# Layer norms before tensor-multiplied units: low parts of input tiles 6 and 7 moved from VectorE to GpSimd

## The chip, the core and the metric

One NeuronCore of a Trainium2 chip runs the whole program. The metric is the device time in microseconds from the first to the last instruction of one execution, with what lies around it; less is better. The kernel before takes 1235.99 us, the median of three runs (1234.67 to 1236.5).

## What is computed

Three transformer layers on a sequence of 256 tokens of width 1024, in float32. The first layer uses RMS norms. The other two are "hybrid" layers that use layer norms, and these are what the change touches:

```python
def layer_norm(x, g, b):
    mu = jnp.mean(xf, axis=-1, keepdims=True)
    var = jnp.mean(jnp.square(xf - mu), axis=-1, keepdims=True)
    y = (xf - mu) * lax.rsqrt(var + LN_EPS)
    return (y * g + b)

def hybrid_layer(x, ...):
    proj = x @ w_in                       # 38 column tiles with the branch merges
    ...
    x = layer_norm(ALPHA * x + mix, ln1_g, ln1_b)
    up = causal_dwconv_2(x @ w_up, ffn_conv_w)
    a, b = jnp.split(up, 2, axis=-1)
    ffn = (silu(a) * b) @ w_down
    return layer_norm(ALPHA * x + ffn, ln2_g, ln2_b)
```

With two such layers there are four layer norms: `ln10`, `ln20` (first hybrid layer), `ln11`, `ln21` (second). The output of the first three feeds a matrix product; `ln21` is the program's output.

## The kernel before

**Layout and precision.** Activations are held transposed: eight tiles (t = 0 to 7) of 128 features x 256 tokens. TensorE multiplies in a reduced float32 format, so every operand is split into a high part (the value rounded) and a low part (the rest), and one 128 x 128 weight block times one activation tile is three matmuls: high x high (L1065), high weights x low activations (L1066), low weights x high activations (L1067). A "unit" is one 512 KB weight tile of eight such blocks, so 24 matmuls.

**The weight stream.** For every unit SP issues the DMA into a ring of three raw buffers, ScalarE makes the high part (`hi_part`, L733), VectorE the low part (`lo_part`, L1391), and TensorE waits for `split_lo`. The DMA of unit n waits for the low part of unit n - 3. Each engine runs a program order written out by hand; semaphores link them.

**A layer norm.** VectorE makes deviations, ScalarE squares them, GpSimd adds them up, TensorE sums over features and spreads mean and inverse deviation over the partitions, with some matmuls on a tile of ones (`warm`, L1081) between. GpSimd then adds the mean to tiles 1 to 7 of `dev` (L694), tile by tile. VectorE follows in `layer_norm`: for s = 0 to 9 it scales tile s with gain and inverse deviation (L1457, semaphore `scaled`) and then makes the low part of tile s - 2, that is `dev + b - high` (L1461 and its continuation, semaphore `x_lo`). ScalarE makes the high parts `dev + b` (L767, `x_hi`). After its loop VectorE goes on to the low part of the next weights (the third unit of the stage), which ScalarE has made ready beforehand.

**What follows it on TensorE.** `ramp` takes the first two units of the next stage together, tile by tile: for each tile k it waits for the low part of tile k (`LOW[which, k]`), then issues the six matmuls of both units. From the third unit on it waits for weights alone.

**What follows it on GpSimd.** `keep` makes the biased tiles `x = dev + b` (L700), which the residual of the next half layer needs much later. For `ln10` and `ln11` the stage after is the FFN's up projection. There GpSimd has to multiply gate and value of every pair of units (L634, semaphore `product`), and ScalarE, in program order, makes the high part of that product (L993) before it makes the high part of the weights of the sixth unit. So the first product stands behind `keep` on GpSimd, and the sixth unit's weights stand behind the first product on ScalarE. For `ln20` the next stage is `win21`, where GpSimd's next step is `pool_sums`, after the copy of the eighth unit.

For the RMS norms GpSimd already makes the low parts of tiles 4 and 6 (`POOL_LOW`, `low_parts`, L667).

Of the kernel before, what the change touches and what calls it, by code (L numbers as in the profile page):

```python
# [12 lines left out]
KT = DM // P  # L13
# [181 lines left out]
def build(nc, args, out):  # L195
    f32, r32, i32 = mybir.dt.float32, mybir.dt.float32r, mybir.dt.int32
    ALU, ACT = mybir.AluOpType, mybir.ActivationFunctionType
    ctx = ExitStack()
    with ctx:
        def sb(name, shape, dt=f32, stack=ctx):  # L200
            return stack.enter_context(nc.sbuf_tensor(name, shape, dt))

        def sem(name):
            return ctx.enter_context(nc.semaphore(name))
# [11 lines left out]
        def tiles_of(n, at_line):  # L216

            out = []
            for t in range(n):
                which = 0 if t in at_line else 1  # L220
                out.append((aligned, shifted)[which][:, placed[which], :])
                placed[which] += 1
            return out
# [6 lines left out]
        xhi, xlo = tiles_of(KT, (0,)), tiles_of(KT, (0,))  # L230
        yhi, ylo = tiles_of(16, (2, 8)), tiles_of(16, (2, 8))
        x = sb("x", [P, KT, S])
# [45 lines left out]
        def statistic(c, n=2):  # L278
            return stats[:, c:c + n]


        def col(name, i=0, n=1):
            a = COLS[name] + i
            return vec[:, a:a + n]

        def cst(name, n):
# [27 lines left out]
        normed_dve, normed_act, x_hi, x_lo, x_lo_pool = (sem(n) for n in ("normed_dve", "normed_act", "x_hi", "x_lo", "x_lo_pool"))  # L314
# [3 lines left out]
        dev_summed, mean_ready, mean_spread, mean_copied, var_ready, recentred, recentred_dve, mean_squared, x_kept = (  # L318
            sem(n) for n in ("dev_summed", "mean_ready", "mean_spread", "mean_copied", "var_ready", "recentred", "recentred_dve", "mean_squared",
                             "x_kept"))  # L320
# [151 lines left out]
        XHI = {n: KT * i for i, n in enumerate(NORMS)}  # L472
# [4 lines left out]
        LNI = {"ln10": 0, "ln20": 1, "ln11": 2, "ln21": 3}  # L477
        RES = {"ffn": 0, "final": KT, "ln10": 2 * KT, "ln20": 3 * KT, "ln11": 4 * KT, "ln21": 5 * KT}


        POOL_LOW = (4, 6)
        NORMED, LOW, tally = {}, {}, {}

        def tell(s):
            tally[s.name] = tally.get(s.name, 0) + 1
            return s, tally[s.name]

        def dve_last(t):

            return t % 2 == 1  # L490

        for n in NORMS:
            for t in range(KT):
                if n not in LNI:
                    NORMED[n, t] = tell(normed_dve)
                elif n == NORMS[-1]:
                    NORMED[n, t] = tell(normed_dve if dve_last(t) else normed_act)
                if n != NORMS[-1]:
                    LOW[n, t] = tell(x_lo_pool if n not in LNI and t in POOL_LOW else x_lo)

        def square_place(t, it):

# [47 lines left out]
        def _(pool):  # L550
# [112 lines left out]
            def low_parts(which, src):  # L663
                for t in POOL_LOW:
                    pool.wait_ge(*NORMED[which, t])
                    pool.wait_ge(x_hi, XHI[which] + t + 1)
                    pool.tensor_tensor(xlo[t], src[:, t, :], xhi[t].bitcast(f32), ALU.subtract).then_inc(x_lo_pool, 1)  # L667

            def add_squares(which):

                for t in range(FIRST_SUMMED if which == "mix" else KT - 1):
                    if which == "mix":

                        pool.wait_ge((squared, dve_squared)[t % 2], t // 2 + 1)
                    else:
                        pool.wait_ge(squared, SQ[which] + t + 1)
                    add_tile(t, 0, dev[:, t, :], dev[:, 0, :], added_q, ACCQ[which])
# [17 lines left out]

            def keep(which):

                for t in range(KT):
                    pool.wait_ge(scaled, KT * LNI[which] + t + 1)
                    pool.tensor_scalar(x[:, t, :], dev[:, t, :], col(which[:3] + "_b" + which[3], t), None, ALU.add).then_inc(x_kept, 1)  # L700

            add_squares("mix")
            low_parts("mix", dev)
# [8 lines left out]
            for l in range(LAYERS2):  # L712
                for n in range(START[f"win2{l}"], START[f"wout2{l}"]):
                    steps(n)
                merge(KT * (1 + l), 1)
                layer_norm(f"ln1{l}")
                keep(f"ln1{l}")
                ffn(1 + l, f"up2{l}")
                layer_norm(f"ln2{l}")
                if l < LAYERS2 - 1:  # L720
                    keep(f"ln2{l}")
# [654 lines left out]
        def _(dve):  # L1376
            count = [0]

            def link(ins):

                count[0] += 1
                ins.then_inc(dve_chain, 1)
                dve.wait_ge(dve_chain, count[0])
# [13 lines left out]
            def on_diagonal(i, c, done):  # L1397

                for h in range(2):
                    ins = dve.tensor_scalar(diag[:, i, h * P:(h + 1) * P], ident, statistic(c + h, 1), None, ALU.mult)  # L1400
                ins.then_inc(done, 1)

            def invert(which, after=None):
                dve.wait_ge(rooted, SUM[which])
                link(dve.reciprocal(statistic(INVERSE), statistic(DEVIATION)))
                on_diagonal(1, INVERSE, inverted)
                if after is not None:
                    lo_part(after)
                if which in LNI:
                    dve.wait_ge(mean_copied, LNI[which] + 1)  # L1410
                    dve.tensor_tensor(dev[:, 0, :], dev[:, 0, :], mean_rows, ALU.add).then_inc(recentred_dve, 1)  # L1411

                dve.wait_ge(spread, SUM[which])

            def low_part(which, t, src):
                if t in POOL_LOW:
                    return
                dve.wait_ge(x_hi, XHI[which] + t + 1)
                dve.wait_ge(*NORMED[which, t])
                low(xlo[t], src[:, t, :], xhi[t], x_lo)  # L1420
# [19 lines left out]
            def layer_norm(which, last):  # L1440
                i = LNI[which]
                dve.wait_ge(dev_summed, i + 1)
                link(dve.tensor_scalar(statistic(NMEAN), dev_sums, -1.0 / DM, None, ALU.mult))
                on_diagonal(0, NMEAN, mean_ready)
                dve.tensor_tensor(statistic(MEAN2), statistic(NMEAN), statistic(NMEAN), ALU.mult).then_inc(mean_squared, 1)
                dve.wait_ge(mean_squared, i + 1)
                dve.wait_ge(summed, SUM[which])
                dve.scalar_tensor_tensor(statistic(VAR), square_sums, 1.0 / DM, statistic(MEAN2), ALU.mult, ALU.subtract).then_inc(var_ready, 1)
                invert(which)
                g, b = which[:3] + "_g" + which[3], which[:3] + "_b" + which[3]  # L1450
                for s in range(KT + 2):
                    if s < KT:
                        if s == 0:
                            dve.wait_ge(recentred_dve, i + 1)
                        else:
                            dve.wait_ge(recentred, (KT - 1) * i + s)
                        dve.scalar_tensor_tensor(dev[:, s, :], dev[:, s, :], col(g, s), spread_inverse, ALU.mult, ALU.mult).then_inc(scaled, 1)  # L1457
                    t = s - 2
                    if t >= 0 and not last:
                        dve.wait_ge(x_hi, XHI[which] + t + 1)  # L1460
                        dve.scalar_tensor_tensor(xlo[t], dev[:, t, :], col(b, t), xhi[t].bitcast(f32), ALU.add, ALU.subtract) \  # L1461
                            .then_inc(x_lo, 1)
                    if last and s >= 1 and s <= KT and dve_last(s - 1):
                        dve.wait_ge(scaled, KT * i + s)
                        dve.tensor_scalar(x[:, s - 1, :], dev[:, s - 1, :], col(b, s - 1), None, ALU.add).then_inc(normed_dve, 1)  # L1465
# [298 lines left out]
            for n in range(WIN1):  # L1764
                if 24 <= PLAN1[n] < 32:

                    t = PLAN1[n] - 24
# [14 lines left out]
            for l in range(LAYERS2):  # L1782
                lo_part(START[f"win2{l}"] + 2)
                waiting, base = None, KT * (1 + l)
                for p, (kind, t) in enumerate(PLAN2):
                    n = START[f"win2{l}"] + p
# [128 lines left out]
```

## Time and profile before

| | |
|---|---|
| median of three runs | 1235.99 us |
| the profiled execution | 1236.2 us, of which the span of instructions is 1234.4 us |
| TensorE matmul busy | 1208.5 us (98%) |
| TensorE weight load busy | 1183.6 us (96%) |
| VectorE busy | 844.7 us (68%) |
| ScalarE busy | 705.9 us (57%) |
| GpSimd busy | 399.6 us (32%) |
| granted TensorE clock, mean | 0.992 |

A timeline row gives the start in us from the span's start, the duration, engine, line, operation, output and inputs, the count of merged instructions, and in brackets the idle time of the engine ahead of it and what released it. Merged rows (x2 and more) span from the first start to the last end. Starts overlap the end of the instruction before on the same engine a little, since engines are pipelined.

### The profile page before, as it was taken

Reading aid. Unit: us, or ns where it says so; the run is one execution under the profiler, and the core shown is the slowest. Engines: PE = TensorE matmul, PEld = TensorE weight load, DVE = VectorE, ACT = ScalarE, POOL = GpSimd, SP = SyncE. Lnnn points to the kernel's source line nnn. Section 1 sums busy time; section 2 is a strip of 40 time slices with the busy share of each in tenths; the row PEclk is TensorE's granted clock in tenths of the full one; section 3 lists DMA queues with packets and bytes.
Section 4 is the critical chain, followed back from the end, with each engine's and each line's share of the span. In section 5 each row is a group of like instructions: output and inputs, shape, how many; then the busy total and the mean of one; then the engine's idle time right before and its main releaser. Section 6 shows DMA issues by size and latency. Waiting matters only on the chain. (4 is left out here: it accounts for less than half of the span.)

```text
span 1234.4 us, 27264 instructions
## 1 busy us (share of the span) xinstructions
PE 1208.5 (98%) x10242; PEld 1183.6 (96%) x10242; DVE 844.7 (68%) x1458; ACT 705.9 (57%) x1228; POOL 399.6 (32%) x376
## 2 busy tenths in 40 slices
PE   8999999999999999999999999999999999999997
PEld 8998989999999999999999999999999999999997
DVE  5867664676777765767677777755766677777655
ACT  4666566545666654466455666644466555666642
POOL 2006214023334402210338434314610339343313
PEclk8999999999999999999999999999999999999999
DMA  6554445665566666454653666565554654566662
GB/s 242 187 166 142 137 133 153 194 191 169 172 188 197 189 192 189 154 158 151 188 174 123 186 187 198 173 205 155 154 171 142 187 180 128 186 190 187 199 190 87
DMA packets 60288, 212.70 MB, mean 172 GB/s; under 512 B 6688, under 2 KB 7968, under 8 KB 60064
## 3 DMA queue, kind: packets, MB, share of 16 engines
q1 hardware_dynamic: 60192, 211.39, 55.8%
q8 instruction: 65, 1.06, 0.4%
q14 instruction: 31, 0.25, 0.1%
HBM read 210.31 MB, written 1.05 MB: 171 GB/s over the span
## 5 line engine op out<-in xcount | busy, mean ns | idle before, releaser
L1391 DVE TENSOR_TENSOR wlo<-raw,whi 128x1024 fp32r<-128x1024 f32 (+1 forms) x400 | 489.5, 1225 | 302.0 <-ACT whi L733 300.0
L1065 PE MATMUL bank<-shifted,whi 128*128 128x256 f32 x2296 | 639.3, 278 | 1.3 <-POOL shifted L667 1.1
L1066 PE MATMUL bank<-shifted,whi 128*128 128x256 f32 x2296 | 636.2, 277 | 0.0
L1067 PE MATMUL bank<-shifted,wlo 128*128 128x256 f32 x2296 | 635.9, 277 | 0.0
L733 ACT ACTIVATE whi<-raw 128x1024 fp32r<-128x1024 f32 (+1 forms) x400 | 415.7, 1040 | 146.7 <-PE bank L1067 134.4
L1065 PEld LDWEIGHTS bank<-shifted,whi 128*128 128x128 f32 x2296 | 431.5, 188 | 3.1 <-POOL shifted L667 1.3
L1067 PEld LDWEIGHTS bank<-shifted,wlo 128*128 128x128 f32 x2296 | 431.7, 188 | 0.0
L1066 PEld LDWEIGHTS bank<-shifted,whi 128*128 128x128 f32 x2296 | 431.1, 188 | 0.0
L634 POOL TENSOR_TENSOR fprod<-ugate,uval 128x256 f32<-128x256 f32 x66 | 99.4, 1506 | 210.1 <-DVE uval L1736 204.5
L1065 PE MATMUL bank<-fhi,whi 128*128 128x256 f32 x528 | 146.1, 277 | 0.0
L1067 PE MATMUL bank<-fhi,wlo 128*128 128x256 f32 x528 | 145.8, 276 | 0.0
L1066 PE MATMUL bank<-flo,whi 128*128 128x256 f32 x528 | 145.8, 276 | 0.0
L648 POOL TENSOR_TENSOR u<-u,tmp 128x256 f32<-128x256 f32 x48 | 53.6, 1118 | 235.8 <-DVE tmp L1691 233.7
L1065 PE MATMUL bank<-aligned,whi 128*128 128x256 f32 x334 | 105.5, 316 | 5.6 <-DVE wlo L1391 3.8
L1065 PEld LDWEIGHTS bank<-fhi,whi 128*128 128x128 f32 x528 | 99.2, 188 | 0.1
L1066 PEld LDWEIGHTS bank<-flo,whi 128*128 128x128 f32 x528 | 99.1, 188 | 0.0
L1067 PEld LDWEIGHTS bank<-fhi,wlo 128*128 128x128 f32 x528 | 99.1, 188 | 0.0
L1067 PE MATMUL bank<-aligned,wlo 128*128 128x256 f32 x334 | 93.3, 279 | 0.0
L1066 PE MATMUL bank<-aligned,whi 128*128 128x256 f32 x334 | 92.5, 277 | 0.0
L993 ACT ACTIVATE fhi<-fprod 128x256 f32 (+1 forms) x66 | 27.6, 418 | 99.8 <-POOL fprod L634 99.8
L1065 PEld LDWEIGHTS bank<-aligned,whi 128*128 128x128 f32 x334 | 62.8, 188 | 16.1 <-issue 8.2
L1066 PEld LDWEIGHTS bank<-aligned,whi 128*128 128x128 f32 x334 | 62.9, 188 | 0.7
(212 smaller groups left out, 1276.4 us busy)
## 6 DMA issues: line engine op xcount, KB each, us to landing
raw<-in_w_win SPq DMA_DIRECT2D x140, 512.0 KB, 3.6
raw<-in_w_up SPq DMA_DIRECT2D x132, 512.0 KB, 3.6
raw<-in_w_down SPq DMA_DIRECT2D x48, 448.0 KB, 3.8
raw<-in_w_merge SPq DMA_DIRECT2D x32, 512.0 KB, 3.9
raw<-in_w_out SPq DMA_DIRECT2D x24, 512.0 KB, 3.6
raw<-in_w_down SPq DMA_DIRECT2D x24, 512.0 KB, 3.6
x<-in_x SPq DMA_DIRECT2D x4, 256.0 KB, 4.6
rgw<-in_rg_w SPq DMA_DIRECT2D x1, 1024.0 KB, 9.8
```

The lines of the kernel that those rows point to most:

```text
L634: pool.tensor_tensor(tile(fprod, t % 3), tile(ugate, t % 3), tile(uval, t % 3), ALU.mult).then_inc(product, 1)
L648: ins = pool.tensor_tensor(m, m, branch_part(base, t, branch), ALU.add)
L733: act.activation(whi[:, n % RING, 0:blocks * P], raw[:, n % RING, 0:blocks * P], ACT.Copy).then_inc(split_hi, 1)
L993: act.activation(tile(fhi, t, it, 3), tile(fprod, t % 3), ACT.Copy).then_inc(f_hi, 1)
L1065: pe.matmul(ps, whi[:, slot, w], hi, start=first, stop=False)
L1066: pe.matmul(ps, whi[:, slot, w], lo, start=False, stop=False)
L1067: return pe.matmul(ps, wlo[:, slot, w], hi, start=False, stop=last)
L1391: dve.tensor_tensor(wlo[:, n % RING, w], raw[:, n % RING, w], whi[:, n % RING, w].bitcast(f32), ALU.subtract) \
```

## The change

A pair of tiles, `KEPT_FIRST = (6, 7)`, gets its low parts on GpSimd in the three layer norms that feed units. `keep` takes tiles 6 and 7 first, then 0 to 5. For 6 and 7 it waits for its own biased tile (`x_kept`) and for ScalarE's high part (`x_hi`), and subtracts. VectorE leaves out its two instructions for these tiles. TensorE's `ramp` waits for `x_lo_pool` instead of `x_lo` at k = 6 and k = 7; the table `LOW` is built to match.

```diff
         POOL_LOW = (4, 6)
+        KEPT_FIRST = (6, 7)
...
-                    LOW[n, t] = tell(x_lo_pool if n not in LNI and t in POOL_LOW else x_lo)
+                    LOW[n, t] = tell(x_lo_pool if t in (KEPT_FIRST if n in LNI else POOL_LOW) else x_lo)
...
             def keep(which):
 
-                for t in range(KT):
+                for t in KEPT_FIRST + tuple(range(KEPT_FIRST[0])):
                     pool.wait_ge(scaled, KT * LNI[which] + t + 1)
                     pool.tensor_scalar(x[:, t, :], dev[:, t, :], col(which[:3] + "_b" + which[3], t), None, ALU.add).then_inc(x_kept, 1)
+                    if t in KEPT_FIRST:
+                        pool.wait_ge(x_kept, KT * LNI[which] + KEPT_FIRST.index(t) + 1)
+                        pool.wait_ge(x_hi, XHI[which] + t + 1)
+                        pool.tensor_tensor(xlo[t], x[:, t, :], xhi[t].bitcast(f32), ALU.subtract).then_inc(x_lo_pool, 1)
...
                     t = s - 2
-                    if t >= 0 and not last:
+                    if t >= 0 and not last and t not in KEPT_FIRST:
                         dve.wait_ge(x_hi, XHI[which] + t + 1)
                         dve.scalar_tensor_tensor(xlo[t], dev[:, t, :], col(b, t), xhi[t].bitcast(f32), ALU.add, ALU.subtract) \
                             .then_inc(x_lo, 1)
```

## Rows read from the trace of the kernel before

**Rows 1.** The page, part 1: busy time of each engine over the span.
```profile
PE 1208.5 (98%) x10242; PEld 1183.6 (96%) x10242; DVE 844.7 (68%) x1458; ACT 705.9 (57%) x1228; POOL 399.6 (32%) x376
```
**Rows 2.** Timelines of PE, and last of PEld, behind ln10, 670 to 684 us.
```profile
672.49 0.28 PE L1065 MATMUL bank<-shifted,whi 128*128 128x256 f32 x1
...
673.20 0.28 PE L1065 MATMUL bank<-shifted,whi 128*128 128x256 f32 x1
...
673.90 0.28 PE L1065 MATMUL bank<-aligned,whi 128*128 128x256 f32 x1
...
683.69 0.19 PEld L1065 LDWEIGHTS bank<-aligned,whi 128*128 128x128 f32 x1 [1.34 <-DVE wlo L1391]
```
**Rows 3.** Timeline of DVE, same stretch: two scalings, low parts, three weight splits.
```profile
669.97 0.47 DVE L1457 SCALAR_TENSOR_TENSOR dev<-dev,vec,bank 128x256 f32<-128x256 f32 x1
...
671.15 1.26 DVE L1461 SCALAR_TENSOR_TENSOR shifted<-dev,vec,shifted 128x256 fp32r<-128x256 f32 x3
672.34 1.21 DVE L1391 TENSOR_TENSOR wlo<-raw,whi 128x1024 fp32r<-128x1024 f32 x1
...
675.21 1.49 DVE L1391 TENSOR_TENSOR wlo<-raw,whi 128x1024 fp32r<-128x1024 f32 x1
...
682.41 1.22 DVE L1391 TENSOR_TENSOR wlo<-raw,whi 128x1024 fp32r<-128x1024 f32 x1 [2.02 <-ACT whi L733]
```
**Rows 4.** Timelines of POOL, same stretch, in windows that single its instructions out.
```profile
664.11 5.66 POOL L694 TENSOR_TENSOR dev<-dev,fprod 128x256 f32<-128x256 f32 x7 [3.13 <-ACT fprod L748]
...
671.73 2.53 POOL L700 TENSOR_SCALAR x<-dev,vec 128x256 f32<-128x256 f32 x1
...
675.15 0.92 POOL L700 TENSOR_SCALAR x<-dev,vec 128x256 f32<-128x256 f32 x1
...
676.05 1.44 POOL L700 TENSOR_SCALAR x<-dev,vec 128x256 f32<-128x256 f32 x1
...
678.38 1.90 POOL L700 TENSOR_SCALAR x<-dev,vec 128x256 f32<-128x256 f32 x1
...
680.24 0.73 POOL L634 TENSOR_TENSOR fprod<-ugate,uval 128x256 f32<-128x256 f32 x1
```
**Rows 5.** Timeline of ACT, same stretch: first product's high part, then sixth unit's weights.
```profile
681.01 0.42 ACT L993 ACTIVATE fhi<-fprod 128x256 fp32r<-128x256 f32 x1 [2.43 <-POOL fprod L634]
681.33 1.04 ACT L733 ACTIVATE whi<-raw 128x1024 fp32r<-128x1024 f32 x1
```
**Rows 6.** Timeline of POOL, 892 to 893 us: two instructions linked by a semaphore.
```profile
892.09 0.80 POOL L581 TENSOR_TENSOR u<-pads 64x256 f32<-64x256 f32 x1
892.97 4.28 POOL L587 TENSOR_TENSOR u<-pads,const 64x256 f32<-64x256 f32 x3
```
**Rows 7.** Timeline ahead of ln10, 657 to 660 us: POOL beside a weight split.
```profile
657.21 0.75 POOL L661 TENSOR_TENSOR acc<-acc,dev 128x256 f32<-128x256 f32 x1
...
657.46 1.57 DVE L1391 TENSOR_TENSOR wlo<-raw,whi 128x1024 fp32r<-128x1024 f32 x1 [0.74 <-ACT whi L733]
...
657.90 1.72 POOL L661 TENSOR_TENSOR acc<-acc,tmp 128x256 f32<-128x256 f32 x1
```
**Rows 8.** Timelines of POOL behind ln20: keep and its next work.
```profile
864.13 11.55 POOL L700 TENSOR_SCALAR x<-dev,vec 128x256 f32<-128x256 f32 x8
...
887.69 4.33 POOL L577 TENSOR_TENSOR pads<-pads 128x542 f32<-128x542 f32 x3 [11.86 <-ACT pads L1040]
```
**Rows 9.** Timelines behind ln11: POOL's keep, and PEld at the sixth unit.
```profile
1038.05 10.59 POOL L700 TENSOR_SCALAR x<-dev,vec 128x256 f32<-128x256 f32 x8
...
1052.06 0.19 PEld L1065 LDWEIGHTS bank<-aligned,whi 128*128 128x128 f32 x1 [1.26 <-DVE wlo L1391]
```
**Rows 10.** Windows: stretch, its length, busy us of PE, PEld, DVE, ACT, POOL, PEclk, DMA.
```profile
662.00:663.00 1.00, 1.00 (x5) 0.91 (x6) 0.35 (x3) 0.15 (x1) 0.00 (x0) 0.50 0.09 33
682.00:684.00 2.00, 0.85 (x7) 0.66 (x7) 1.59 (x2) 2.00 (x5) 0.00 (x0) 1.00 0.28 113
700.00:850.00 150.00, 149.68 (x1302) 149.21 (x1301) 100.48 (x139) 84.18 (x134) 50.82 (x46) 1.00 0.63 190
```

## Prediction

> **What bounds the kernel now.** I read the page's busy times first: TensorE's matmuls are busy for 98% of the span [rows 1], so only what stops TensorE counts. The busy shares by stretch say where it does not stop: between 700 and 850 us it is busy 149.68 of 150 us [rows 10], so nothing there gives a delay back. It stops around the norms. Then I read the timelines of the three places that the change touches (behind ln10 at 665 us, ln20 at 860 us, ln11 at 1034 us), engine by engine. In the ramp, tiles 6 and 7 are not what TensorE waits for: it begins k = 6 at 672.49 us, k = 7 at 673.20 and the third unit at 673.90, 0.70 us apart [rows 2], which is six matmuls back to back. VectorE's last low parts end at 672.41 (1.26 us from 671.15) and the weight split for the third unit at 673.55 [rows 3], 0.35 us before TensorE wants it. The stop that is left comes later: at the sixth unit TensorE is idle for 1.34 us until 683.69, by its weight load [rows 2], because the split at 682.41 waited for ScalarE [rows 3], ScalarE waited 2.43 us for GpSimd's first product [rows 5], and GpSimd had been in `keep` until 680.24 [rows 4]. The same stands behind ln11, with 1.26 us until 1052.06 [rows 9]. So GpSimd is the engine on the path in two of the three places, and it is the one that gets more work.
>
> **What is removed.** Two of VectorE's eight low parts per norm, 0.39 us each by the pitch of the three in 1.26 us [rows 3]: its next split begins at 671.54 instead of 672.34 and ends at 672.75. This moves nothing: TensorE wants it at 673.90 and had it in time already. What the earlier end could release is the DMA of a later unit, whose buffer is filled long before use. Gain: nothing. Were the 0.35 us of slack not there, it would be worth at most 0.8 us for each of three norms.
>
> **What is added to the ramp.** Tiles 6 and 7 now come from GpSimd, in a chain of four instructions. For ln10:
> - GpSimd is free at 669.77 (5.66 us from 664.11 [rows 4]), but has to wait for tile 6 scaled, at 670.44 (669.97 + 0.47 [rows 3]). Start 670.5: 0.7 us idle that `keep` did not have while it began with tile 0.
> - Biased tile 6: 0.92 us, the length of a `keep` instruction that nothing disturbs (675.15 [rows 4]), so until 671.4. ScalarE's high part is made in the meantime.
> - A dependent instruction starts 0.08 us after the end of the one before (892.09 + 0.80 to 892.97 [rows 6]): 671.5.
> - The subtraction takes 0.73 us undisturbed, like the product [rows 4]. But VectorE is then in a low part and starts its weight split right behind it, at 671.54. How GpSimd fares beside it: an addition begun at 657.90, inside a split that ran from 657.46 to 659.03, took 1.72 us and ended 0.59 us behind it [rows 7]; the `keep` instruction of 671.73 took 2.53 us and ended 0.71 behind the split [rows 3, 4]. So it ends about 0.65 us after 672.75: 673.4.
> - Biased tile 7 until 674.3, 0.08 us, subtraction until 675.1. Nothing of VectorE with two inputs in SBUF runs then, since its next split hangs on TensorE's first unit.
> - TensorE starts k = 6 at 673.5 and k = 7 at 675.2 instead of 673.20: **2.0 us late**, in two stops of about 1.0 us.
>
> Bounds: with no disturbance at all the chain ends at 674.0 (670.5 + 2 x (0.92 + 0.08 + 0.73)), 0.9 us late. With another 1.0 us of blocking in the second pair it is 3.0. I take 2.0 since the split's start is fixed by VectorE's own order.
>
> A rule speaks to the one step I am least sure of. Rows 7 show both orders: the addition of 657.21, begun ahead of the split, took its 0.75 us and the split was stretched to 1.57; the one begun inside it waited. The Trainium skill, "SBUF — State Buffer", section "Who interferes with whom", says that a VectorE instruction with two SBUF inputs and a GpSimd one that reads SBUF exclude each other and that the first to start keeps the port pair. By that rule, a subtraction that gets in before 671.54 ends at 672.2 and VectorE waits; the low part that VectorE is in at 671.5 speaks for the other order here. The `keep` of 671.73 started before its split and was held all the same, which fits only if it was already waiting behind low parts.
>
> **ln20.** The same chain; GpSimd starts `keep` at 864.13 there and is busy with it for 11.55 us [rows 8], against 10.5 behind ln10. Nothing behind it depends on `keep`: GpSimd is idle for 11.86 us before its next real work [rows 8], which hides the longer loop; were that cover gone, its 2.4 us would count. TensorE's 2.0 us stay: **+2.0 us**.
>
> **ln10 and ln11, up to the sixth unit.** Here two shifts meet, and the later one counts. TensorE itself comes 2.0 us late, less the stop of 1.3 us that it had: +0.7. Against this stands GpSimd's first product. From the last subtraction (675.1, call it E) come six `keep` instructions at a pitch of 0.90 and then the product. VectorE's fourth unit split follows TensorE's first unit: before, it came 2.0 us behind k = 7 (673.20 to 675.21 [rows 2, 3]), so now at E + 2.1, and the fifth one 3.0 us later, E + 5.1. One begun just ahead of a split passes unharmed and the next waits (675.15 with 0.92 us, then 676.05 with 1.44, beside the split of 675.21 [rows 3, 4]). So: three instructions until E + 2.7, the fourth held until E + 4.1, two more until E + 5.9, the product held by the fifth unit's split until E + 7.15: 682.25. Before, it ended at 680.97 (680.24 + 0.73). That is 1.3 us later, and product, high part, weights' high part, split and TensorE follow each other without a gap [rows 5, 3, 2]. **+1.3 us each**, of which the 0.7 is a part. If the product itself is not held: +0.8. By plain addition (0.7 idle + 2 x 0.08 + 2 x 0.73, with as much holding as before, where three instructions lost 1.6, 0.5 and 1.0 us [rows 4]) it is 2.3, and 2.8 with one hold more.
>
> **Sum.** 2.0 + 1.3 + 1.3 = 4.6 us on the profiled execution's 1236.2, so 1240.8; that execution lies 0.2 above the median of the runs, so **1240.6 us**, +0.37%. Other queues are untouched: no DMA is issued or moved, ScalarE's order is the same. Readers of the biased tiles come a whole stage later.
>
> **Rivals.**
> - **The subtraction slips in before the split** (the point that decides is whether it starts before about 671.5, or GpSimd's four instructions run with no hold). Then the ramp is 0.9 us late; in ln10 and ln11 this is inside the old stop of 1.3, and if the product is also not later than before, they cost 0 to 0.3. Sum 0.9 to 1.5 us: 1237.1 us, not slower by more than 0.2%. For it: 657.21 [rows 7]. Against: 0.7 us of waiting for tile 6 puts the start beside VectorE's back to back work. It would take the good case in all three. Chance 0.13.
> - **GpSimd's loop counts in full.** The product is 2.3 to 2.8 us late, since the holds fall badly, as they did before. Sum 2.0 + 2 x 2.5 = 7.0: 1243.0 us. For it: three holds in 10.5 us before. Chance 0.22.
> - **The clock falls in the ramp's two stops.** In the norm's thin stretch it was at 0.50, 1.2 GHz, in 662 to 663 us [rows 10]. Against: the stop at 682 to 684, with TensorE busy 0.85 of 2 us, left it at 1.00. Were a fall to last 4 us (an estimate, four such stretches), it would lose 2.0 us behind ln20; behind ln10 and ln11 GpSimd's lateness covers much of it. Sum 4.6 + 2.0 + 2 x 0.6 = 7.8: 1243.8 us. Chance 0.09.
> - **VectorE's earlier end is worth something** that these rows don't show and GpSimd is in time: three times 0.3 us saved, 1235.1. Chance 0.03.
>
> **How the numbers follow.** My forecast has 0.53. The measurement can tell 0.2%, about 2.5 us, from no change, so the border is 1238.5. Slower: the forecast, less 0.02 for its low end, and the two dearer rivals, 0.82. Within: 0.13 + 0.02 and what of the last rival stays inside, 0.16. Faster by over 0.2%: 0.02. Range: from 1237.8 (between the first rival and the ramp's lower bound with small product delays) to 1244.2 (beyond both dear rivals' centres).
>
> **What the profile after would show.** Right: in the ramps TensorE idle twice for about 1 us, at k = 6 and k = 7, released by GpSimd's new subtraction; a first subtraction of 1.7 us or more; GpSimd's first product ending about 1.3 us later and the stop at the sixth unit still there, 0.6 longer than the ramp leaves room for. Wrong: no wait of TensorE for GpSimd in the ramp, a first subtraction of 0.73 us, or a stop at the sixth unit as short as before with the product in its old place. If the product moves by 2.5 us, the placing of the holds was wrong; if the granted clock is under 1 behind the ramp, the clock's rival is true.

## The result

| | us |
|---|---|
| before, median of 7 runs | 1235.99 (1234.67 to 1237.78) |
| changed, median of 7 runs | 1239.79 (1238.31 to 1241.30) |
| ratio | 1.0036, 95% interval 1.0026 to 1.0045 |
| span of the profiled executions | 1234.4 and 1236.5 |

The change costs 3.8 us by the medians, 3.2 to 5.6 us by the interval. The forecast was 4.6 us. The first lines of the changed kernel's page hardly show it (they answer to [rows 1]; the last line is from the page's list of costliest groups):

```profile
PE 1207.5 (98%) x10242; PEld 1181.5 (96%) x10242; DVE 843.6 (68%) x1452; ACT 706.5 (57%) x1228; POOL 400.4 (32%) x382
...
L1070 PE MATMUL bank<-shifted,whi 128*128 128x256 f32 x2296 | 639.2, 278 | 6.0 <-POOL shifted L705 4.5
```

Busy times are the same within 2.1 us; what is new is idle time ahead of a matmul, with GpSimd's new line L705 as what ended it.

### The profile page after: what moved, and what is told of

Its sections match the earlier page's. It is cut to its first block and busy times, and to the rows that moved or that the text cites. A ratio compares the mean times of both kernels' runs of the same rounds, so it can differ in the third digit from the quotient of the medians.

```text
span 1236.5 us, 27270 instructions
## 1 busy us (share of the span) xinstructions
PE 1207.5 (98%) x10242; PEld 1181.5 (96%) x10242; DVE 843.6 (68%) x1452; ACT 706.5 (57%) x1228; POOL 400.4 (32%) x382
```

## Where the time went, read in the trace

**How the stretches are compared.** The two spans differ by 2.1 us and not by 3.8, since single executions also differ where the code is the same. The changed one is 2.0 us ahead already at `ln10`'s first sum (658.4 us against 660.4), which lies before all that the change touches; I have not looked for the reason. A further 1.0 us comes from the three thin stretches from a norm's first sum to its first scaling, 4.58, 4.66 and 4.57 us against 5.28, 5.28 and 4.24: where the granted clock stays at 1.00 such a stretch takes 4.2 us, where it falls to 0.50, up to 5.3. So I don't compare absolute times, but times from one fixed point, the start of VectorE's scaling of tile 6 (L1457 before, L1462 after). It is ahead of all that the change touches.

VectorE behind `ln10` in the changed kernel, the answer to [rows 3]:

```profile
667.32 0.47 DVE L1462 SCALAR_TENSOR_TENSOR dev<-dev,vec,bank 128x256 f32<-128x256 f32 x1
...
668.50 0.48 DVE L1466 SCALAR_TENSOR_TENSOR shifted<-dev,vec,shifted 128x256 fp32r<-128x256 f32 x1
668.89 1.22 DVE L1396 TENSOR_TENSOR wlo<-raw,whi 128x1024 fp32r<-128x1024 f32 x1
...
681.05 1.23 DVE L1396 TENSOR_TENSOR wlo<-raw,whi 128x1024 fp32r<-128x1024 f32 x1 [1.12 <-ACT whi L738]
```

Two low parts are gone; the split for the third unit starts 1.57 us behind the scaling of tile 6 instead of 2.37 [rows 3]. GpSimd in the same stretch, the answer to [rows 4]:

```profile
667.89 1.10 POOL L701 TENSOR_SCALAR x<-dev,vec 128x256 f32<-128x256 f32 x1 [0.77 <-DVE dev L1462]
669.07 1.62 POOL L705 TENSOR_TENSOR shifted<-x,shifted 128x256 fp32r<-128x256 f32 x1
670.68 0.92 POOL L701 TENSOR_SCALAR x<-dev,vec 128x256 f32<-128x256 f32 x1
671.68 0.72 POOL L705 TENSOR_TENSOR shifted<-x,shifted 128x256 fp32r<-128x256 f32 x1
672.38 6.02 POOL L701 TENSOR_SCALAR x<-dev,vec 128x256 f32<-128x256 f32 x6
678.37 1.25 POOL L635 TENSOR_TENSOR fprod<-ugate,uval 128x256 f32<-128x256 f32 x1
```

The reader sees the whole chain of the forecast: 0.77 us idle for tile 6, the biased tile, 0.08 us, a subtraction of 1.62 us that ends 0.58 us behind the split (669.07 + 1.62 against 668.89 + 1.22), then a pair that nothing disturbs, its subtraction in 0.72 us. The first biased tile takes 1.10 us and not the 0.92 of the forecast; this costs nothing, since the subtraction is held until the split is over in either case. Six `keep` instructions take 6.02 us, one of them held, and the product 1.25, held by a split. TensorE's weight loads that had to wait, behind `ln10`, `ln20` and `ln11` (answers to [rows 2] and [rows 9]):

```profile
670.75 0.19 PEld L1070 LDWEIGHTS bank<-shifted,whi 128*128 128x128 f32 x1 [0.97 <-POOL shifted L705]
672.46 0.19 PEld L1070 LDWEIGHTS bank<-shifted,whi 128*128 128x128 f32 x1 [0.96 <-POOL shifted L705]
679.08 0.19 PEld L1070 LDWEIGHTS bank<-aligned,whi 128*128 128x128 f32 x1 [0.36 <-DVE wlo L1396]
682.33 0.19 PEld L1070 LDWEIGHTS bank<-aligned,whi 128*128 128x128 f32 x1 [0.43 <-DVE wlo L1396]
...
865.80 0.19 PEld L1070 LDWEIGHTS bank<-shifted,whi 128*128 128x128 f32 x1 [0.96 <-POOL shifted L705]
867.51 0.19 PEld L1070 LDWEIGHTS bank<-shifted,whi 128*128 128x128 f32 x1 [0.94 <-POOL shifted L705]
...
1043.15 0.19 PEld L1070 LDWEIGHTS bank<-shifted,whi 128*128 128x128 f32 x1 [0.95 <-POOL shifted L705]
1044.86 0.19 PEld L1070 LDWEIGHTS bank<-shifted,whi 128*128 128x128 f32 x1 [0.95 <-POOL shifted L705]
1051.47 0.19 PEld L1070 LDWEIGHTS bank<-aligned,whi 128*128 128x128 f32 x1 [0.38 <-DVE wlo L1396]
1054.72 0.19 PEld L1070 LDWEIGHTS bank<-aligned,whi 128*128 128x128 f32 x1 [0.43 <-DVE wlo L1396]
```

Each ramp has two new stops of 0.94 to 0.97 us, at tiles 6 and 7. Behind `ln10` and `ln11` the old stop of 1.34 and 1.26 us at the sixth unit is now 0.43, with 0.36 and 0.38 at the fifth (behind `ln11` the kernel before had 0.32 there already): the stop moved ahead, and the sixth unit's weights came later all the same.

The table gives, for each kernel's profiled execution, the start of a unit's first weight load less the start of the scaling of tile 6, in us (for the changed kernel's sixth unit behind `ln10`: 682.33 - 667.32 = 15.01).

| kernel | ln10: third | ln10: sixth | ln20: third | ln20: fifth | ln11: third | ln11: sixth |
|---|---|---|---|---|---|---|
| before | 3.82 | 13.72 | 3.76 | 10.03 | 3.75 | 13.78 |
| changed | 5.84 | 15.01 | 5.83 | 12.09 | 5.82 | 15.00 |
| ln20_only | 3.77 | 13.77 | 5.84 | 12.20 | 3.82 | 13.71 |
| ups_only | 5.83 | 15.01 | 3.82 | 10.18 | 5.99 | 15.77 |
| order_only | 3.77 | 14.67 | 3.75 | 10.02 | 3.77 | 14.68 |
| no_lows | 3.82 | 12.99 | 3.75 | 10.01 | 3.76 | 12.93 |
| split_waits | 5.51 | 15.65 | 5.50 | 11.85 | 5.51 | 15.66 |
| keep_later | 3.75 | 12.46 | 3.74 | 10.04 | 3.76 | 12.49 |
| change_keep_later | 5.83 | 14.60 | 5.81 | 12.07 | 6.01 | 15.65 |

Changed less before: 1.29 at the sixth unit behind `ln10`, 2.06 at the fifth behind `ln20`, 1.22 at the sixth behind `ln11`, together 4.6 us.

This is not yet the cost up to the next norm. From the scaling of tile 6 to the next norm's first sum the three stages take 186.13, 168.44 and 184.56 us, before 184.84, 165.00 and 183.88: 1.29, 3.44 and 0.68 us longer, together 5.4. So 1.4 us are added behind `ln20` after the fifth unit, about 0.5 each at the fourteenth and the twenty-fifth, and 0.5 us are given back behind `ln11`. The 1.4 us are not in every execution: in `ln20_only`, with the same code in that stage, it takes 167.24 us, 2.2 more than before. What adds them is not settled.

## The experiments

### One norm or two at a time

`ln20_only` and `ups_only` are the changed kernel with the pair of tiles given by norm. `ln20_only` is shown; in `ups_only` the names are `ln10` and `ln11`. The table `LOW` and `keep` ask the same function:

```diff
+        def kept_first(which):
+            return KEPT_FIRST if which in ('ln20',) else ()
...
-                    if t >= 0 and not last and t not in KEPT_FIRST:
+                    if t >= 0 and not last and t not in kept_first(which):
```

> The change in the norm before win21 alone; ln10 and ln11 as before. My theory: GpSimd's chain of four stops TensorE twice in that ramp, about 1.0 us each, and nothing behind it takes this back, so +2.0 us in total and 2.0 us more from the scaling of tile 6 to the third unit's first matmul (3.87 us before). Rival, that a ramp's delay is partly taken back by slack further on in the stage: under 1 us in total. Rival, that only the up projections cost: 0.

Measured: 1237.58 us against 1235.34 for the kernel before on the same chip, ratio 1.0016 (1.0006 to 1.0026), so 2.2 us by the medians. The third unit behind `ln20` is 2.08 us later, the fifth 2.17, and the other norms are as before. Up to the next norm's first sum the stage is 2.2 us longer (167.24 against 165.00 us), so nothing is given back. The rivals of under 1 us and of 0 fall by the trace; by the time alone 0.7 us would still be inside the interval.

> The change in ln10 and ln11 alone. My theory: each costs 1.3 us at the sixth unit, since GpSimd's first product comes that much later and the ramp's 2.0 us fall into the old stop of 1.3; +2.6 us in total; from the scaling of tile 6 to the sixth unit's first weight load 15.0 us where it was 13.7. Rival, that the ramps' delays count in full: 2 x 2.0 = 4.0 us.

Measured: 1236.85 us, ratio 1.0015 (1.0006 to 1.0025), 1.5 us by the medians; the 2.6 us of my theory are inside the interval (0.7 to 3.1). The sixth unit behind `ln10` is at 15.01, as expected, though the third is 2.01 us late: the ramp's delay is swallowed by the old stop, and the product's is what is left. The rival (4.0 us) is outside the interval. Behind `ln11` it is at 15.77, and the reason is the clock. The windows of this kernel behind its two stops there (stretch, length, busy us of PE, PEld, DVE, ACT, POOL, PEclk, DMA share, GB/s):

```profile
1042.00:1043.00 1.00, 0.91 (x6) 0.91 (x7) 0.00 (x0) 0.24 (x1) 1.00 (x3) 0.78 0.72 291
1043.00:1044.00 1.00, 1.00 (x6) 1.00 (x6) 0.69 (x2) 1.00 (x2) 1.00 (x2) 0.50 0.00 0
1044.00:1045.00 1.00, 1.00 (x7) 1.00 (x6) 1.00 (x2) 0.98 (x3) 1.00 (x2) 0.50 0.00 0
1045.00:1046.00 1.00, 1.00 (x7) 1.00 (x6) 0.96 (x3) 0.99 (x2) 1.00 (x1) 0.51 0.00 0
1046.00:1047.00 1.00, 1.00 (x10) 1.00 (x10) 0.35 (x1) 1.00 (x2) 1.00 (x2) 1.00 0.17 45
```

That is the rival of the clock, in one ramp: at 1.2 GHz for about 3 us, 6 or 7 matmuls in a microsecond instead of 10. The third unit takes 4.20 us instead of 2.74, 1.4 us more, of which 0.76 is left at the sixth unit.

### The order alone

```diff
-                for t in range(KT):
+                for t in (6, 7) + tuple(range(6)):
                     pool.wait_ge(scaled, KT * LNI[which] + t + 1)
```

> The kernel before with only the order of the biased tiles changed, 6 and 7 first; all low parts stay with VectorE. My theory: the ramps are as before, with no stop; GpSimd idles 0.7 to 0.8 us for tile 6, and its first product comes 0.7 to 1.2 us later, so each up projection's sixth unit is 0.7 to 1.2 us later: 1.4 to 2.4 us in total, nothing behind ln20. Rival, that the two added subtractions alone make the product late: 0 here.

Measured: 1237.23 us, ratio 1.0015 (1.0006 to 1.0025), 1.9 us by the medians. No wait in any ramp; the sixth unit is 0.95 and 0.90 us later, its stop 2.23 us where it was 1.34:

```profile
682.85 0.19 PEld L1065 LDWEIGHTS bank<-aligned,whi 128*128 128x128 f32 x1 [2.23 <-DVE wlo L1391]
```

So the waiting for tile 6 alone makes most of what the up projections lose. The rival falls. Behind `ln11` the longer stop had a second effect in this execution: the granted clock fell to 0.50 about 1.2 us after it, for some 3 us, and the seventh unit starts 4.15 us behind the sixth instead of 2.75; behind `ln10` the same stop of 2.23 us left the clock at 1.00.

### What VectorE saves, alone

```diff
-                    if t >= 0 and not last:
+                    if t >= 0 and not last and t < 6:
```

In this kernel TensorE waits for the high part of tiles 6 and 7 instead (`LOW[n, t] = (x_hi, ...)`).

> The kernel before without the low parts of tiles 6 and 7 in the three layer norms: nobody makes them, so those matmuls multiply an old low part. This is what VectorE saves and nothing else. My theory: its weight split comes 0.8 us earlier and TensorE does not wait for it, so 0 (within 0.3 us). Rival, that VectorE's time behind the norm is worth something: up to 0.8 us for each norm, 2.4 us faster.

Measured: 1233.34 us, ratio 0.9985 (0.9975 to 0.9994): 2.0 us faster. My theory falls and its rival's size is met, but not its place: the third unit starts as before behind all three norms (3.82, 3.75, 3.76), and nothing is gained behind `ln20`. The gain is at the sixth unit, 0.73 and 0.85 us. GpSimd shows why:

```profile
669.05 9.28 POOL L703 TENSOR_SCALAR x<-dev,vec 128x256 f32<-128x256 f32 x8
678.29 1.25 POOL L637 TENSOR_TENSOR fprod<-ugate,uval 128x256 f32<-128x256 f32 x1
```

Its eight biased tiles take 9.28 us, before 10.5 from 669.75 to 680.24 [rows 4]. The `keep` instruction of 2.53 us at 671.73 ran beside VectorE's last low parts and the split behind them, and ended only 0.71 us behind the split. Without two of the low parts the same instruction takes 1.83 us and ends 0.7 us sooner against the scaling of tile 6, the first product ends 0.7 us sooner, and the sixth unit starts sooner with it. The run `keep_later_no_lows` below tests this.

### Is it the split that holds the subtraction?

The changed kernel, with one wait more at the end of VectorE's loop:

```diff
+                if not last:
+                    dve.wait_ge(*LOW[which, KT - 1])
```

> The changed kernel, but VectorE begins its weight split behind the norm only when GpSimd has made tile 7's low part. This takes the split away from beside GpSimd's first subtraction. My theory (the split holds that subtraction for 0.9 us): the subtraction takes 0.73 us instead of 1.62, tile 7's low part comes 0.9 to 1.1 us earlier, and the third unit is then short of its weights by about 0.5 us, since the split ends only 1.3 us behind the low part; behind ln20 +1.4 us to the kernel before instead of 2.0; the first product no later than in the kernel before or up to 0.4. In total +1.5 to +2.5 us to the kernel before. Rival, that GpSimd's subtraction takes 1.6 us by itself: its length is unchanged, the third unit comes 1.3 us later still, and the total is +6 or more.

Measured: 1242.3 us against 1235.14, ratio 1.0059 (1.0043 to 1.0075), 7.2 us slower than before. The local part came out as my theory said. GpSimd behind `ln10`, and TensorE's waits:

```profile
670.66 1.10 POOL L701 TENSOR_SCALAR x<-dev,vec 128x256 f32<-128x256 f32 x1 [0.78 <-DVE dev L1462]
671.85 0.74 POOL L705 TENSOR_TENSOR shifted<-x,shifted 128x256 fp32r<-128x256 f32 x1
...
673.57 0.72 POOL L705 TENSOR_TENSOR shifted<-x,shifted 128x256 fp32r<-128x256 f32 x1
674.27 8.07 POOL L701 TENSOR_SCALAR x<-dev,vec 128x256 f32<-128x256 f32 x6
682.31 0.73 POOL L635 TENSOR_TENSOR fprod<-ugate,uval 128x256 f32<-128x256 f32 x1
```
```profile
674.35 0.19 PEld L1070 LDWEIGHTS bank<-shifted,whi 128*128 128x128 f32 x1 [0.96 <-POOL shifted L705]
675.61 0.19 PEld L1070 LDWEIGHTS bank<-aligned,whi 128*128 128x128 f32 x1 [0.50 <-DVE wlo L1396]
685.75 0.19 PEld L1070 LDWEIGHTS bank<-aligned,whi 128*128 128x128 f32 x1 [1.75 <-DVE wlo L1396]
```

```profile
674.33 1.23 DVE L1396 TENSOR_TENSOR wlo<-raw,whi 128x1024 fp32r<-128x1024 f32 x1 [2.58 <-POOL shifted L705]
...
676.46 1.33 DVE L1396 TENSOR_TENSOR wlo<-raw,whi 128x1024 fp32r<-128x1024 f32 x1
...
679.50 1.23 DVE L1396 TENSOR_TENSOR wlo<-raw,whi 128x1024 fp32r<-128x1024 f32 x1 [0.80 <-ACT whi L738]
```

The subtraction takes 0.74 us instead of 1.62, with the same instruction and the same data: the split held it for 0.9 us. The stop at tile 6 is gone and the third unit is short of its weights for 0.50 us, as expected. The total was missed by far, for a reason that my theory left out: the holding is not avoided, only moved. Now three splits, the last three rows, lie beside the six `keep` instructions and hold three of them (1.99, 1.44 and 1.97 us instead of 0.92); in the changed kernel one split held one (1.50 us). The six take 8.07 us instead of 6.02, and the sixth unit comes 1.93 and 1.88 us late. The rival falls on the subtraction's length, though it was nearer in the total. By the table the three places make 5.6 to 5.7 us of the 7.2 (1.93, 1.82 at the fifth unit, 1.88); the rest is inside the interval's 5.3 to 9.3 (four runs of this kernel).

### Taking the loop away from the first product

In the kernel before, half of the biased tiles of `ln10` and `ln11` are made between the products; `change_keep_later` does the same to the changed kernel, with tiles 6, 7, 0 and 1 first. `rest` is a call that GpSimd's part of the FFN makes behind its first and its second product (of the diff only the calls are shown, those of `keep_later`).

```diff
                     if t or not isinstance(it, int):
                         low(t - 1, it)
+                    if isinstance(it, int) and i in (1, 3):
+                        rest((4, 5) if i == 1 else (6, 7))
...
-                keep(f"ln1{l}")
-                ffn(1 + l, f"up2{l}")
+                keep(f"ln1{l}", (0, 1, 2, 3))
+                ffn(1 + l, f"up2{l}", lambda tiles, l=l: keep(f"ln1{l}", tiles))
```

> The kernel before, but in ln10 and ln11 only tiles 0 to 3 get their bias ahead of the first product; 4 and 5 follow the first product, 6 and 7 the second. My theory (the loop in front of the first product makes the stop of 1.3 us at the sixth unit): the stop goes, 2.5 us faster in total, if GpSimd's later products have room for it (3 us idle between them). Rival, that the stop then comes from another step (ScalarE's table load, the fifth unit's split): under 1 us faster.

> keep_later once more, on the same chip as the two above. By the stages of its trace (2.1 us less behind ln10 and ln11 each, 0.7 more behind ln20) it should be 3.1 us faster than the kernel before, though it measured 4.9; where it comes out says which of the two is nearer.

Measured: 1230.26 us against 1235.14, ratio 0.9962 (0.9949 to 0.9976), and on a second occasion 1229.75 against 1235.06, 0.9954 (0.9940 to 0.9967). **This version beats both kernels, by 4.9 and 5.3 us on the one before and by some 9 on the changed one, by the ratios to the kernel before.** GpSimd, and TensorE's only wait behind `ln10`:

```profile
669.43 5.42 POOL L702 TENSOR_SCALAR x<-dev,vec 128x256 f32<-128x256 f32 x4
677.06 0.74 POOL L634 TENSOR_TENSOR fprod<-ugate,uval 128x256 f32<-128x256 f32 x1 [2.20 <-DVE uval L1738]
677.77 2.35 POOL L702 TENSOR_SCALAR x<-dev,vec 128x256 f32<-128x256 f32 x2
```
```profile
679.38 0.19 PEld L1067 LDWEIGHTS bank<-aligned,whi 128*128 128x128 f32 x1 [0.42 <-DVE wlo L1393]
```

Now the product waits for VectorE, and the sixth unit's weights no longer wait for the product; the stop at the sixth unit is gone, and it starts 1.26 and 1.29 us earlier. The mechanism is right, the size was too small: up to the next norm the up and down projections behind `ln10` take 2.07 us less, not 1.26. Most of the other 0.8 us is gained between the sixteenth and the thirty-seventh unit, which follow each other mostly at 2.74 us here and at 2.74 to 2.9 before. What sets that pace is not settled. On the question of the second text: the terms that it lists make 3.5 and not 3.1 us. From the scaling of tile 6 to the next norm's first sum the three stages are 3.4 us shorter in total than before in the first execution (2.06 less, 0.48 more, 1.77 less), and 4.4 in the second (2.09 less, 0.19 more, 2.50 less). So single executions differ by 1 us here, and the medians' 4.9 and 5.3 lie above both.

> The changed kernel, with only tiles 6, 7, 0 and 1 ahead of the first product in ln10 and ln11, 2 and 3 behind the first and 4 and 5 behind the second. My theory (two shifts that meet at the sixth unit, the later counts): with the product in time, the ramps' delay of 1.9 us is what is left. To keep_later this kernel is 3 x 1.9 = 5.7 us slower; to the kernel before 2 x 0.6 + 1.9 = 3.1 us slower, so 1.3 us faster than the change. Rival, that the changed kernel's loss in the up projections is made in the ramp and not by the product: the same as the change, +3.8 to +4.5.

Measured: 1239.52 us, ratio 1.0036 (1.0023 to 1.0050), 4.4 us slower than before and no faster than the change, so in the total the rival is met. The trace of one execution says: behind `ln10` the sixth unit is at 14.60, 0.41 earlier than in the changed kernel and 0.88 later than in the kernel before (0.6 expected), with no stop of its own; behind `ln20` as in the changed kernel; behind `ln11` at 15.65 and not 14.6, since the clock fell to 0.50 behind the ramp's two stops, for some 3 us, as in `ups_only`. Up to the next norm the stage behind `ln10` is only 0.08 us longer than before. So the local mechanism holds, and the clock took part of the gain here; how often it falls cannot be said from single profiles, and why the median is 9.3 us above `keep_later` where 5.7 was expected stays open in part.

### Two steps further from keep_later

> keep_later without the low parts of tiles 6 and 7 (an old low part is multiplied). Taking them away made the kernel before 2.0 us faster, which I had not expected. My theory now: it acts only through GpSimd, whose third biased tile is no longer held by VectorE's last low parts, so its first product comes 0.8 us earlier; where the product is in time anyway it is worth nothing: the same as keep_later within 0.5 us, sixth unit at 12.5 us behind the scaling of tile 6. Rival, that VectorE's earlier weight split is what counts: 1.6 to 2.0 us faster than keep_later, here too.

Measured: 1229.96 us (ratio to the kernel before 0.9955, 0.9941 to 0.9969), where `keep_later` on the same chip took 1229.75: no gain. The sixth unit is at 12.52 behind `ln10`. The two low parts that are worth 2.0 us in the kernel before are worth nothing where GpSimd's product is in time. GpSimd's third biased tile takes 1.82 us instead of 2.54 here too, but the product waits for VectorE, so nothing follows from it. So the saving acts through the time of GpSimd's product, and its rival, 1.6 to 2.0 us from the earlier split, falls.

```diff
                 norm_shift(f"ln1{l}", False)
+                load_table(ACT.Silu)
```

> keep_later, with ScalarE loading the table of Silu behind its high parts, where it idles 1.98 us, instead of at the first Silu of each up projection. My theory: the stop of 0.42 us at the fifth unit is made by the 1.28 us of that load, so it goes, 0.4 us for each of two: 0.8 us faster than keep_later, and the fifth unit 9.2 to 9.3 us behind the scaling of tile 6 where it is 9.72. Rival, that the load is hidden by another wait: the same as keep_later.

Measured: 1230.20 us (ratio 0.9957, 0.9943 to 0.9971), the same as `keep_later`. The local part of my theory is right: the load of 1.28 us lies in ScalarE's idle time, the fifth unit is at 9.41 and 9.26 instead of 9.73 and 9.78 with no wait, the sixth at 12.15 and 12.00. But up to the next norm's sums nothing is left of it (182.98 us from the scaling of tile 6 behind `ln10`, 182.78 and 182.75 in the two executions of `keep_later`): the 0.3 us are given back between the twentieth and the thirty-seventh unit. I did not find by what.

## Why the prediction was right

- **The ramp, 2.0 us in two stops of about 1.0: right.** Measured 2.02, 2.07 and 2.07 at the third unit, stops of 0.94 to 0.97.
- **The first subtraction held until 0.65 us behind the split: right.** It took 1.62 us (the prediction's sign was 1.7 or more) and ended 0.58 us behind. It began 0.2 us later than forecast, since the biased tile took 1.10 us; the split's end set its end, so that error had no effect. `split_waits` shows that the split is the cause, with 0.74. The first rival, that it slips in ahead, did not happen in any of the nine ramps in which both could meet (`ln20_only`, `ups_only`, the changed kernel and `change_keep_later`).
- **ln20: 2.0 expected, 2.06 at the fifth unit.** `ln20_only` measured 2.2. In the changed kernel's own profile the whole stage is 3.44 us longer; the prediction has no term for the other 1.4.
- **"Nothing there gives a delay back", from 149.68 of 150 us busy [rows 10]: not safe.** Matmuls that count as busy can still follow each other more slowly: behind `ln10`, units 15 to 37 take 61.25 us before and 60.38 in `keep_later`.
- **The sixth unit, 1.3 us for each up projection: right in size.** Measured 1.29 and 1.22, and the order in which the holds fall was right too: product 1.25 us after 6.02 us of `keep`. `order_only` and `no_lows` split the term into parts: 0.95 and 0.90 for beginning with tile 6, minus 0.73 and 0.85 for VectorE's two low parts, so 1.1 to 1.2 is left for the two subtractions with their holds, if the parts add up.
- **"This moves nothing": wrong.** The step looked only at TensorE's wait for the split and priced VectorE's saving at nothing. It is worth 2.0 us by itself, through GpSimd's held instruction [rows 3, 4]. The sum was not hurt, because the product's time was worked out instruction by instruction from the new place of the split; had it been made by adding parts, this one would have been missing.
- **The clock in the ramp, given a chance of 0.09: it exists.** It fell in two of the nine ramps with both stops (`ups_only` and `change_keep_later`, both behind `ln11`), and in none of the changed kernel's own profile. How often it falls in the runs without a profile is not known.
- **The total.** The terms are 2.0 + 1.3 + 1.3 = 4.6, the three places in the trace give 4.6, the stages up to the next norm 5.4, the medians 3.8 with an interval of 3.2 to 5.6. So each term is borne out at its place; that their sum meets the places to 0.1 us is closer than the totals can tell.

## What to carry to other kernels

Before work moves to an engine that is "32% busy", look at what stands behind it in that engine's queue: here a loop whose result was needed a stage later stood ahead of a product that the weights of the sixth unit hung on, and moving half of that loop gained 5 us (of which 2.5 are seen at the sixth unit) where moving two instructions onto the engine lost 4. A wait that two paths share takes the later of the two delays and not their sum, so both have to be followed to it. And time that one of VectorE and GpSimd saves has to be looked for in the other one, since they hold each other up.

## What the runs showed of the hardware

- An addition, subtraction or product of 128 x 256 on GpSimd takes 0.71 to 0.75 us alone. Begun inside a 1.2 us split of VectorE (two inputs in SBUF) it ends about 0.6 us behind the split: 1.62 us for the first subtraction, 1.25 for the product begun later in its split, 1.72 in [rows 7]. A `keep` instruction, 0.92 us alone, ends 0.7 to 0.8 us behind the split that held it.
- A GpSimd instruction that begins ahead of a split delays it by less than its own length. All the traces give the same sums: for 26 `keep` instructions of 0.92 us begun 0.06 to 0.31 us ahead of a split, head start plus what the split takes over 1.22 us is 0.32 to 0.34 us, and for 169 GpSimd instructions with two inputs (0.71 to 0.76 us long, begun 0.2 to 0.55 us ahead) it is 0.58 to 0.61 us. With more head start the split takes its 1.22 us: the `keep` of 674.19 in the changed kernel, 0.38 us ahead, left the split of 674.58 at 1.22. The Trainium skill, "SBUF — State Buffer", section "SBUF: two separate sides", has the pair of ports held for the whole instruction by the first to start; in these rows the split is kept off for 0.33 and 0.60 us from that instruction's start.
- At the short end the order turns. Nine `keep` instructions that began 0 to 0.06 us ahead of a split were held themselves, for 1.96 to 1.99 us, and left the split at 1.23 to 1.25; two that began 0.06 us ahead, that of 675.15 [rows 4] among them, went through. The first two rows are of the changed kernel, the others of `split_waits`:

```profile
677.48 0.92 POOL L701 TENSOR_SCALAR x<-dev,vec 128x256 f32<-128x256 f32 x1
677.62 1.41 DVE L1396 TENSOR_TENSOR wlo<-raw,whi 128x1024 fp32r<-128x1024 f32 x1 [0.91 <-ACT whi L738]
...
674.27 1.99 POOL L701 TENSOR_SCALAR x<-dev,vec 128x256 f32<-128x256 f32 x1
674.33 1.23 DVE L1396 TENSOR_TENSOR wlo<-raw,whi 128x1024 fp32r<-128x1024 f32 x1 [2.58 <-POOL shifted L705]
```

- Two stops of TensorE of 0.95 us, 0.75 us apart, were followed by a fall of the granted clock to 0.50 for about 3 us in two of nine cases. In all nine the stops were the same. What differed was the norm's thin stretch ahead of the ramp: in both cases with a fall the clock had stayed at 1.00 all through it, and in six of the seven others it had been at 0.50 for about 3 us there, within 10 us ahead of the scaling of tile 6. The seventh (`ups_only` behind `ln10`) had neither fall, so this is an observation and not a rule.
